# Even layer's projections: three of the products as seven block products in place of eight, and the last tile's norm by halves

## What is computed

```
h = rmsnorm(x, norm_mix[0])
z = h @ w_in_even[0]          # (1152, 1024) @ (1024, 3596)
fq, fk, fv, ff, mqk, mv, mo, mi, mf = split(z)   # 512 512 512 8 1024 512 512 4 4 columns
...
y = rmsnorm(x, norm_final)    # returned as y_prompt (1024 rows) and y_sample (128 rows)
```

## Time and profile before

| | us |
|---|---|
| median of 3 runs | 2833.42 (2829.95 to 2835.3) |
| the profiled execution | 2835.96 |
| its span, first to last instruction | 2834.1 |

### The profile page before, as it was taken

One profiled execution on the slowest core, in us unless ns is written; L12 is line 12 of the kernel. 1 busy time (PEld: TensorE's weight loads), 2 busy tenths in 40 slices (PEclk: granted clock), 3 DMA queues, 4 the chain that ended last, 5 costly groups with the idle time before them and its releaser, 6 DMA issues.

```text
span 2834.1 us, 43348 instructions
## 1 busy us (share of the span) xinstructions
PE 2734.7 (96%) x17102; PEld 2501.2 (88%) x17102; DVE 1556.7 (55%) x2105; ACT 1024.6 (36%) x1633; POOL 1301.4 (46%) x750
## 2 busy tenths in 40 slices
PE   7999999898989999999999999999999999999998
PEld 7999988786888899988998988987878999899997
DVE  5500227666466776667754320088367666776665
ACT  5422436454343333333324310366253333333233
POOL 2112355333365665656632231276446565655652
PEclk9999999999999999999999999999999999999999
DMA  4111230144284355544542131032565554355541
GB/s 142 45 45 56 96 115 25 63 133 140 85 276 159 138 218 203 186 164 143 207 155 106 45 127 64 1 127 68 193 181 213 203 196 166 144 193 203 209 175 68
DMA packets 189533, 388.13 MB, mean 137 GB/s; under 512 B 26629, under 2 KB 144737, under 8 KB 178916
## 3 DMA queue, kind: packets, MB, share of 16 engines
q1 hardware_dynamic: 179344, 346.94, 35.2%
q0 software_dynamic: 9936, 39.37, 3.7%
q10 hardware_dynamic: 132, 0.13, 0.0%
HBM read 329.58 MB, written 56.79 MB: 136 GB/s over the span
## 4 chain that ended last, share of the span: by engine, by line
PE 79%; DVE 5%; issue 4%; ACT 4%; POOL 4%; DMA 3%; PEld 1%; PEldq 0%; POOLq 0%; SPq 0%; DVEq 0%; ACTq 0%
PE ps L929 23%; PE ps L1007 22%; PE ps L551 16%; PE ps L612 5%; PE ps L1089 3%; PE ps L561 3%; PE ps L2393 1%; DMA units_r<-operands 1%; POOL units_r L688 1%; POOL split L279 1%; PE ps L2711 1%; DMA raw<-w_in_even 1%; POOL split L694 1%; DMA operands<-split 0%; PEld ps L551 0%
## 5 line engine op out<-in xcount | busy, mean ns | idle before, releaser
L1284 POOL TENSOR_TENSOR split<-raw,split 128x1024 fp32r<-128x1024 f32 x218 | 566.9, 2611 | 493.6 <-ACT split L1137 466.0
L929 PE MATMUL ps<-units_r,split 128*128 128x288 f32 x5376 | 720.5, 295 | 18.5 <-DVE units L1375 9.1
L929 PEld LDWEIGHTS ps<-units_r,split 128*128 128x128 f32 x5376 | 716.8, 188 | 22.6 <-POOL split L1284 9.3
L551 PE MATMUL ps<-units_r,split 128*128 128x384 f32 x2736 | 479.0, 335 | 0.7 <-PEq L299 0.7
L551 PEld LDWEIGHTS ps<-units_r,split 128*128 128x128 f32 x2736 | 475.2, 188 | 1.7 <-PEq L299 1.3
L1137 ACT ACTIVATE split<-raw 128x1024 fp32r<-128x1024 f32 x218 | 228.5, 1056 | 456.6 <-PE ps L929 182.0
L1399 DVE TENSOR_TENSOR units<-units,ps 128x512 f32<-128x512 f32 x434 | 285.4, 683 | 121.8 <-PE ps L1007 120.6
L1007 PE MATMUL ps<-split,units_r 128*128 128x512 f32 x1344 | 309.2, 389 | 0.0
L1007 PEld LDWEIGHTS ps<-split,units_r 128*128 128x128 f32 x1344 | 252.3, 188 | 52.4
L279 POOL TENSOR_TENSOR split<-raw,split 128x2048 fp32r<-128x2048 f32 x30 | 138.9, 4630 | 345.4 <-ACT split L274 344.7
L1007 PE MATMUL ps<-split,spare_r 128*128 128x512 f32 x1008 | 235.7, 389 | 0.0
(11 more groups left out here) (490 smaller groups left out, 3732.0 us busy)
## 6 DMA issues: line engine op xcount, KB each, us to landing
units_r<-operands SPq DMA_DIRECT2D x76, 2304.0 KB, 8.8
raw<-w_ff SPq DMA_DIRECT2D x128, 512.0 KB, 4.4
raw<-w_in_even SPq DMA_DIRECT2D x14, 1024.0 KB, 5.2
raw<-w_in_odd SPq DMA_DIRECT2D x12, 1024.0 KB, 5.2
operands<-units_r SPq DMA_DIRECT2D x22, 512.0 KB, 3.8
operands<-split SPq DMA_DIRECT2D x18, 512.0 KB, 4.0
raw<-w_out SPq DMA_DIRECT2D x8, 1024.0 KB, 11.3
units<-x_prompt SPq DMA_DIRECT2D x3, 1536.0 KB, 11.8
```

Of the source, the lines that this page charges most:

```text
L551: last = pe.matmul(ps[:, bank + n, 0:GN], weights(slab, a, k, c0, P), h[b][:, k, n * GN:(n + 1) * GN], start=(k == 0 and q == 0), stop=(k ...
L929: last = pe.matmul(ps[:, bank + f, 0:HN], right_slot(base, slot, a)[:, COLS * k + P * f:COLS * k + P * (f + 1)], x[:, b, k, HN * g:HN * (g ...
L1284: pool.tensor_tensor(right_slot(base, slot, 1), src, right_slot(base, slot, 0), ALU.subtract).then_inc(lo_ready, 1)
```

## The change

Slabs now come in the order `mqk` (0 to 3), gates (4), `mo` (5, 6), `fk` (7, 8), `fq` (9, 10), `fv`, `mv` (11 to 14), and the gate job is job 8. The three outputs `mo`, `fk`, `fq` are passes 0, 1, 2. Each is written as a 2 x 2 product of blocks (512 features x 576 rows times 512 features x 256 columns) and made with seven block products, "slots" 1 to 7. A slot is two calls of `summed_half` (g = 0, 1), 24 matmuls of 288 columns each. Pass 1 takes the operands in the reverse order (`backward`), so that operands that are already in place serve twice.

The combinations of quarters of `h` are made during jobs 0 to 7: on DVE three values in two parts (`difference3_value`, `sum2_value`, `difference4_value`: 3, 2 and 2 instructions of 1,152 columns) and their low parts (`sum_low`), on POOL one value in two parts (3 instructions each) and its low part, high parts on ACT. SP stores them and two plain quarters to `operands`; during the passes it loads 2.25 MB over a quarter of `h` at a time (twelve such loads, the last two bring back the plain quarters for `fv` and `mv`). `mo` is stored by ACT's queue, `proj_tm`'s first nine tiles go in the order 5, 6, 7, 8, 4, 0, 1, 2, 3. The last tile of the final norm is squared, scaled and stored in two halves, on ACT and its queue and on DVE and SP's queue.

In the diff below the parts stand in this order: DVE's and POOL's sums during jobs 0 to 7; ACT's jobs, the first pass's start and the gates; PE's passes and the turn into `proj_tm`; SP's loads (the one under `n == 7` stands between `load(7)` and `load(8)`); DVE's weight sum between two passes, which stands ahead of its adds of slot 6; the last tile.

```diff
+            conv(0)
+            difference3_value(0)
+            conv(1)
+            sum2_value(0)
+            sum_low(0)
+            conv(2)
+            difference4_value(0)
+            sum_low(1)
+            conv(3)
+            difference3_value(1)
+            sum_low(2)
+            conv(4)
+            sum2_value(1)
+            sum_low(3)
+            conv(5)
+            difference4_value(1)
+            sum_low(4)
+            conv(6)
+            sum_low(5)
...
+            dve.tensor_tensor(quarters_of[0][2], quarters_of[0][2], quarters_of[0][3], ALU.add).then_inc(ff_hi, 1)
+            conv(7)
...
+            difference1_value(0)
+            lo_of(pool, 2)
+            difference1_low(0)
+            difference1_value(1)
+            lo_of(pool, 3)
+            difference1_low(1)
+            lo_of(pool, GATES0)
...
+            for j in range(KC):
                 if j % 2 == 0 and j >= 2:
                     hi_of(act, j // 2 + 1)
+                if j in (2, 4):
+                    difference1_high(j // 2 - 1)
+                if j >= 2:
+                    sum_high(j - 2)
                 act.wait_ge(fm_ready, j + 1)
...
+                if j == KC - 1:
+                    act.wait_ge(raw_in[SUMMED0 % 2], raw_count(SUMMED0))
+                    act.wait_ge(slab_begun, SUMMED0)
+                    act.activation(summed_slot(1, 0), quarters_of[0][1], ACT.Copy).then_inc(hi_ready, 1)
+                if j >= 1:
                     silu(j - 1)
...
+            weight_summed(0, 1)
+            summed_high(0, 2, quarters_of[0][2])
             act.wait_ge(gate_ready, 1)
             act.wait_ge(gate_in, 64)
+            act.wait_ge(cb_back[2], 64)
             act.activation(as_groups(M_LOG), ps[64:68, 0:3, 0:GN], ACT.Identity, bias=gbias[0:4, 2:3])
...
+            for g in range(2):
+                act.wait_ge(ff_h, 1 + g)
+                act.activation(part_of(MO_OUT, 0, 0, g), row_sums(g, SET_A), ACT.Copy).then_inc(ff_relu, 1)
+                if g == 0:
+                    summed_high(0, 3, quarters_of[0][0])
+            weight_summed(0, 2)
+            summed_high(0, 4, quarters_of[0][2])
+            silu(KC - 1)
...
+            def summed_half(i, q, r, g, banks, more=False):
+                t = slice(HALF * r + HN * g, HALF * r + HN * (g + 1))
+                for f in range(2):
+                    for k in range(4):
+                        for n, (a, b) in enumerate(PASSES):
+                            last = pe.matmul(ps[:, banks[g] + f, 0:HN],
+                                             summed_slot(i, a)[:, COLS * k + P * f:COLS * k + P * (f + 1)],
+                                             h[b][:, 4 * q + k, t], start=(not more and k == 0 and n == 0),
+                                             stop=(k == 3 and n == 2), skip_group_check=more)
...
+            def forward(p):
+                weight_made(p, 1)
+                for g in range(2):
+                    if p:
+                        added(1, 9 + g)
+                    else:
+                        pe.wait_ge(fm_taken, KC)
+                    summed_half(1, 1, 0, g, SET_A)
+                weight_made(p, 2)
+                for g in range(2):
+                    if p == 0 and g == 0:
+                        upper_half_in(1)
+                    if p == 0 and g == 1:
+                        pe.wait_ge(fk_out, 32)
+                    copied(p, 1 + g)
+                    summed_half(2, 0, 1, g, SET_A)
...
+                weight_made(p, 4)
+                lower_in(2 * p + 1)
+                for g in range(2):
+                    added(p, 1 + g)
+                    summed_half(4, 1, 0, g, SET_B, True)
...
+            added(2, 6)
+            copied(2, 8)
+            upper_half_in(5)
             for j in range(4 * NT):
+                if j == 4:
+                    lower_in(7)
+                tm_job(j, V0 + j // NT, v_tile(j), 0)
...
+            def first_pass_in():
+                sp.wait_ge(gate_ready, 1)
...
+                half_in(UPPER1, 0, 1, upper_in, slice(0, HN))
+                half_in(UPPER1, 0, 1, fk_out, slice(HN, HALF))
+                sp.wait_ge(cb_back[1], 32)
+                summed_rows(0, 2)
+                half_in(MIXED2, 1, 0, mixed_in)
...
+                if n == 7:
+                    sp.wait_ge(cb_back[2], 64)
+                    summed_rows(0, 8)
+                    half_in(MIXED4, 1, 0, mixed_in)
...
+            def backward_first(p):
+                q11, q12, q21, q22 = quarters_of[p]
+                slabs_in(p)
+                dve.tensor_tensor(q21, q11, q21, ALU.subtract).then_inc(ff_hi, 1)
...
+            def last_tile_act(act, own, count):
...
+                link(act, act_own, own, act.activation(junk[:, 512:D], x[:, PT, 512:D], ACT.Square, scale=D ** -0.5,
+                                                       accum_out=ssum[:, PT:NT]))
...
+                link(act, act_own, own, act.activation(last_rows[:, 0:512], last_rows[:, 0:512], ACT.Copy, scale=rstd[:, PT:NT]))
+                act.dma_start(last_out[:, 0:512], last_rows[:, 0:512]).then_inc(seq_in[0], 16)
```

More of the change, by code:

```diff
@@ L3258, in conv, with value_made, difference3_value @@
                                 conv_seq(j)[:, :, STEP:STEP + 3]).then_inc(conv_done, 1)
-            for j in range(KC):
-                conv(j)
+            def value_made(count):
+                dve.wait_ge(ff_y, count)
+            def difference3_value(part_):
+                value = DIFF3[1]
+                if part_:
+                    dve.wait_ge(cb_back[0], 16)
+                after(dve.tensor_tensor(value, normed(1, 1, 0, part_), normed(0, 1, 0, part_), ALU.subtract))
+                after(dve.tensor_tensor(value, value, normed(1, 1, 1, part_), ALU.add))
+                dve.tensor_tensor(value, value, normed(0, 1, 1, part_), ALU.subtract).then_inc(ff_y, 1)
@@ new lines, in sum_low @@
+            def sum_low(k):
+                high, value, low = (DIFF3, SUM2, DIFF4)[k % 3]
+                value_made(k + 1)
+                dve.wait_ge(ff_add, HIGH_AT[k])
+                dve.tensor_tensor(low, value, high, ALU.subtract).then_inc(ff_lo, 1)
+            conv(0)
[8 more added lines that the diff above has]
+            difference3_value(1)
@@ new lines, in weight_made, with slabs_in, summed_add @@
+            def weight_made(p, i):
+                dve.wait_ge(lo_ready, summed_done(p, i))
+            def slabs_in(p):
+                for n in (SUMMED0 + 2 * p, SUMMED0 + 2 * p + 1):
+                    dve.wait_ge(raw_in[n % 2], raw_count(n))
+            def summed_add(p, rows, copy, c, r, banks, more=None):
+                for g in range(2):
+                    dve.wait_ge(ff_h, 14 * p + rows + g)
+                    dve.wait_ge(ff_relu, 8 * p + copy + g)
+                    for c_, r_, taken in ((c, r, None),) if more is None else ((c, r, more), (1, 1, None)):
+                        if taken is not None:
+                            dve.wait_ge(ff_sq, ADDS0[p] + taken + g)
+                        out, src = part_of(SUMMED[p], c_, r_, g), row_sums(g, banks)
+                        if SUMMED_SCALE[p] == 1.0:
+                            dve.tensor_tensor(out, out, src, ALU.add).then_inc(ff_sq, 1)
+                        else:
+                            dve.scalar_tensor_tensor(out=out, in0=src, scalar=SUMMED_SCALE[p], in1=out, op0=ALU.mult,
+                                                     op1=ALU.add).then_inc(ff_sq, 1)
```

546 lines of the change are left out of this document (447 added, 99 removed).

## The result

The kernel after takes 2816.32 us (median of 6 runs, 2814.54 to 2818.79), the kernel before beside it 2834.75 us (6 runs, 2829.95 to 2838.78): ratio 0.9936, 95% interval 0.9926 to 0.9946. That is 18.4 us less, where 8.4 was forecast: right in direction, inside the whole range of 2816 to 2832 by 0.3 us, outside the forecast's own range of 2821 to 2828, and at the value of the rival *No crowding*. The experiments show that the rival's reason was nevertheless not the one, so that the time lies inside the range partly by luck.

The account below looks back on a forecast made before the run. PE, busy 96% of the span, was taken to bound the kernel. Terms: 15.8 + 1.7 - 1.1 - 7.6 - 1.5 - 0.6 + 1.7 = 8.4 us less, forecast 2825.0 us, range 2816 to 2832.

Parts of the forecast that it names:

- No crowding: Rival: in jobs 0 to 7 DVE and POOL turns cost little or late parts have slack; 2816 to 2817.5 us, chance 0.19.
- Products: Rewritten stage on PE: 864 matmuls of 384 columns removed, 1008 of 288 added; saves 15.8 us if PE never waits.
- The stall at 303 us: PE's stop in `proj_tm` before 303.12 us goes, since the gates leave PSUM three passes earlier; saves 1.7 us.
- The turn: Start of `proj_tm`: PE waits for ACT's copy of slot 7's second half; costs 1.1 us.
- Sums of `h` and what is late next: Jobs 0 to 7: DVE and POOL block each other, delaying store, gates and copy; PE waits before slot 2, 7.6 us lost.
- ACT's copy as the releaser: Sign of being right: PE idle before slot 2 ends with ACT's copy; idle 5 to 8 us between 120 and 160 us.
- a DVE instruction of 1,152 columns near 4 us: Sign of being right: DVE's instructions of that width take near 4 us where POOL is at work.
- Clock: After PE's wait of 4 to 7 us the clock can halve; costs 1.5 us, bounds 0 and 3.
- Loads of operands: SP's loads during the passes are nearly hidden, the first having least cover; costs 0.6 us, bounds none to 5.
- Late operands: Rival: nine loads inside the passes each a bit late, 5 us in all, on top of the crowding; 2830 us, chance 0.17.
- The handover between passes: Rival: load and slab come late, PE waits 7 us at each of three handovers; 12.6 us slower, 2846, chance 0.12.
- Last tile: Final norm's last tile in halves: shorter square and scaling, smaller store off POOL's queue; saves 1.7 us, bounds 0.8 and 2.5.

Follow-up runs that it names:

- old tail: Kernel after with the last tile's norm as before (whole tile, one store from POOL's queue): 2820.35 us, ratio 0.9954 to the kernel before.

## Why the prediction was right in direction and less than half the size

The time is inside the range by 0.3 us, and only since the range was drawn down to the value of *No crowding*. The saving of 18.4 us is above the 16 to 17.5 that this rival gave; with the ratio measured and the median of 2833.42 that the forecast started from, the time would be 2815.3, just outside. The terms one by one:

**Products**: 15.8 forecast. In the second profile of after, without a fall of the clock, they save 249.68 - 237.35 = 12.3 us net (the fourth, 237.42, is like it; the third, 238.24, has two more short stops of 0.37 and 0.31 us); with the two waits (2.53 and 0.79 there) added back 15.6. The pace taken from the MLP held.

**The stall at 303 us**: 1.7 forecast. `proj_tm` takes 106.4 us in all profiles of after and 108.2 in those of before, 1.8. **The turn**: 1.1 forecast, 0.79 measured.

**Sums of `h` and what is late next** is the step that failed, in size: 7.6 us forecast, 2.51 measured. By links: DVE starts 0.8 us sooner, at 52.74; laid end to end the work was put at 94.3 us, with 3 us of gaps, and is 91.4 with none. By DVE's timeline 59.8 of it are its own instructions at the pace that they have alone (seven convolutions of 4.77 us and 26.4 of sums; 61.5 forecast), and 31.6 are added beside POOL's (32.8 forecast). So the last low part ends 6.7 us sooner than forecast. Against that the store takes 5.2 us from the end of that part to the gates, not 4.3; the gates and the copy take 4.5, 4.65 in the forecast. PE gets to slot 2 at 151.5, not 152.4. So 160.0 became 153.9 and 152.4 became 151.5. A wait is a difference of two large times; 6.7 us of error in one chain of 97 us is most of the term. The kind was right, and the two experiments on POOL's load show that: each microsecond put on or taken off POOL moved DVE's end by about 0.9 to 1.0, and 16 us more undid nearly the whole change. Of the signs that were named, ACT's copy as the releaser and the rest at 303 us came; a DVE instruction of 1,152 columns near 4 us did not (those of the sums took 1.34 to 1.36, it was the convolution's products that stood), nor did 5 to 8 us of idle PE. *No crowding* was right by its number, not by its reason: DVE is the late engine in the kernel after.

The Trainium skill (SBUF — State Buffer, "SBUF: two separate sides") gives the exclusive lock that the prediction weighed. The trace agrees, also where both queues are full, as in the rows at 65 to 74 us, which the trace before could not show: the engines take turns, an instruction of one for one of the other.

**Clock**: 1.5 forecast. It is a chance, not a cost, as the windows of the kernel after behind the wait show, in its first and its second profile:

```profile
154.00:159.00 5.00, 4.99 (x26) 0.66 1.06 406
```

```profile
154.00:159.00 5.00, 4.51 (x34) 1.00 1.06 406
```

PE had stood for 2.5 us ahead of both, and the clock was at its upper level, 1.00 (2.4 GHz), through that wait. In the first it then was at the lower level, 0.50 (1.2 GHz), for most of the time from 155 to 159 us, which makes the mean of 0.66. The first lost 1.4 us by it (238.74 against 237.35), the second nothing. Of the five profiles with that wait (after's four, old tail) two show it.

**Loads of operands**: 0.6 forecast, no wait of its own in the kernel after, but 1.5 us in the experiment that takes the copies first: it lay under the other. The prediction's case against *Late operands* had a misreading: 1,024 KB in 5.2 us is 197 KB per us, not the same rate as 2,304 KB in 8.8 us, 262. Still, **Late operands** and **The handover between passes** didn't come: PE has no wait at any of the three handovers, though the slabs of `w_in_even` now take 9.0 us where they took 5.2. The slack that they had was not measured.

```profile
units_r<-operands SPq DMA_DIRECT2D x76, 2304.0 KB, 8.9
...
units_r<-operands SPq DMA_DIRECT2D x22, 1152.0 KB, 7.8
raw<-w_in_even SPq DMA_DIRECT2D x14, 1024.0 KB, 9.0
```

**Last tile**: 1.7 forecast; 1.3 against the kernel before (64.1 and 62.8 us, in all seven profiles), 1.4 against the old tail. The square with root and inverse saves 0.3, the scaling 0.6; from its end to the end of the span it is 4.1 us in place of 4.7, 0.5 less, where the prediction had 0.7 without a row.

By measured terms: 15.6 + 1.8 - 0.8 - 2.5 + 1.3 = 15.4, with the 0.7 in front of the output product 16.1; a clock that falls takes up to 1.4 off. The mean span of three profiles before less that of four after is 2832.4 - 2815.0 = 17.4, and the runs give 18.4 with 15 to 21 by the interval. The means of the table place the 17.4: 11.7 in the products, 1.8 in `proj_tm`, 1.2 in attention and mLSTM, 2.3 in the rest, of which 1.3 are the tail, and 0.3 in the start. So 14.8 us lie in the parts that the change rewrites. Attention and mLSTM scatter by 5 to 6 us for the same code, so that their 1.2 can be chance; what makes the 1.0 left in the rest, and the 1 us between 17.4 and 18.4, stays open.

## What to carry to other kernels

A wait forecast as the difference of two long chains needs its own range: put the error of the longer chain (here 7%) on it, not a share of the wait. When a wait is found, look for all that hangs on the same late instruction, here the store, the gates and the first load, and move that instruction; an order on one of its followers (the copies ahead of the gates) uncovers the next. And compare stages, by profiles of the unchanged kernels too, before the last 2 or 3 us of a difference of two spans are given a cause.

## What the runs showed that was not expected

- The granted clock behind one and the same wait of 2.5 us had a mean of 0.66 over 5 us in one execution of the kernel after and stayed at 1.00 in the other three. In attention and the mLSTM, where nothing was edited, one piece of code takes 274.5 to 280.9 us, and 5 to 6 of these are PE's own busy time, longer where the granted clock was lower.
- DVE and POOL lose almost nothing between turns: DVE works for 91.4 us without a gap, POOL's instructions among its own, where 94.3 plus gaps were reckoned.
- When POOL's load made PE stand still for 10.53 us, the clock was at 0.50 before it started again, and the matmuls behind the later wait of 4.48 us ran at that level too:

```profile
101.00:106.00 5.00, 0.00 (x0) 0.50 0.30 120
106.00:111.00 5.00, 4.75 (x19) 0.66 0.30 119
...
169.00:174.00 5.00, 5.00 (x22) 0.50 1.05 406
```

  Products took 254.00 us there, 16.6 more than in the kernel after's second profile, of which the waits are 12.5 (10.53 + 4.48 + 0.79 less 2.53 + 0.79); the other 4 us are the clock's: the 288 matmuls behind the first wait take 51.62 us where as many before it take 50.16, and the 960 behind the second 130.05 where the second profile of after has 127.60.
- A median load of 1,152 KB of operands takes 7.8 us and one of 2,304 KB 8.9: half the bytes save an eighth of the time. The smaller ones are those of this stage, issued in pairs with slabs and stores beside them, so one waits in part for the other; the larger ones are the MLP's.
